# Seven products instead of eight for six of the eight output tiles in each layer's last feed-forward block

## The chip, the core and the metric

The kernel runs on one core of one Trainium2 chip. The metric is the device time of one execution in microseconds (us), lower is better. The engines named below are PE (TensorE, matrix products), DVE (VectorE), ACT (ScalarE), POOL (GpSimd, nearly unused here) and SP (SyncE, which issues the loads).

## The reference

A two-layer encoder trunk over 528 positions (16 meta tokens and 512 frames) of width 1024, all in fp32. Layer 0 mixes by a causal convolution and pooling, layer 1 by gated linear attention. What the change touches is the feed-forward block at the end of each layer and what follows it:

```python
def squared_relu_mlp(u, w1, w2):
    a = jax.nn.relu(u @ w1)
    return (a * a) @ w2
...
        u = rms_norm(h, ffn_norm_g[i])
        h = h + squared_relu_mlp(u, ffn_w1[i], ffn_w2[i])
    return rms_norm(h[:, N_META:], final_norm_g)
```

`ffn_w1` is 1024 x 4096 and `ffn_w2` is 4096 x 1024 in each layer.

## The kernel before

**Products.** Activations lie with channels on the 128 partitions and tokens along the free axis. Each fp32 product is made of three: both operands are split into a high part (rounded to fp32r by ACT) and the rest (a subtraction on DVE), and PE adds hi x lo, hi x hi and lo x hi. One output tile (128 channels) over 1024 input channels is 8 x 3 products. In layer 0 it covers 528 tokens as two matmuls of 264 columns each (48 matmuls); in layer 1 it covers the 512 frames in one matmul (24 matmuls of 512 columns).

**Feed-forward.** The 4096 inner channels are worked in four blocks (`fb` 0 to 3). The first half of a block makes eight tiles of `relu(u @ w1)` (slots `("ffn", layer, fb, 0..7)`), the second half multiplies their squares by the block's part of `w2` and adds the eight result tiles (`8..15`) to `h`. PE writes into four slots of PSUM, `NS = 4`, each of two banks, in the order that `plan_slots` writes out by hand; `start_slot(n)` waits until slot n-4 has been read out.

**Blocks 0 to 2** (`paired_ffn`) take the second half in four pairs of output tiles. A pair is a 2 x 2 block product (two halves of the input channels and tiles by two halves of the tokens) made by seven products instead of eight, Strassen-Winograd. It needs sums of the weights (`pair_sums`, four DVE subtractions or additions into `s_sum`), sums of the squares (`T1` to `T4` beside the four squares `E1, O1, O2, E2`, in `parts8`, split into `c_hi`, `c_lo`), and between the products three copies and a seed on ACT (`seed`, the two `kept` copies, `low`) and three additions into `h` on DVE (`late`, `add_pair` twice). A pair takes 7 x 4 x 3 = 84 matmuls of 264 (layer 0) or 256 columns (layer 1). While PE works on pair p, ACT and DVE split the weights of pair p+1 (`pair_hi`, `pair_lo`, groups 0 to 3); a group's units may be overwritten once PE has done the product that reads them. `parts8` has two buffers, for one pair of first-half tiles each, and ACT's first square of a pair waits for the rests of the pair two before.

**Block 3** (`ffn`) makes all eight result tiles whole, from `a_hi` and `a_lo` (squares, split). After each result tile of layer 0 comes `prep(2, k)`: ACT writes `u_hi` and the squares `h_sq` of the next norm, DVE the rest `u_lo` and the running sum `sq_sum`. In layer 1 ACT's `result` writes `h_sq` and `h` times the final gain into `relu`, PE transposes that tile by four 128 x 128 transposes (`flip_y`), and DVE copies them to `y_tok` (`copy_y`). The last two tiles of layer 1 are made in two halves of 256 tokens each (`end`), followed by the last norm and the output. After layer 0 PE goes on with `project_r` and the first `v` tile, whose weights (`B_V`) are split at the end of block 3.

Every engine runs its instructions in the order in which they are written.

Of the kernel before, what the change touches and what calls it, by code (L numbers as in the profile page):

```python
# [80 lines left out]
PAIRED = FBLK - 1  # L81
# [6 lines left out]
def pair_block(b):  # L88

    first = B_F1 if b >= B_F1 else B_F0  # L90
    return 0 <= b - first < 8 * PAIRED and (b - first) % 8 >= 4

# [12 lines left out]
def plan_slots():  # L105
# [16 lines left out]
    def ffn(layer, norm):  # L122
        for fb in range(FBLK):
            for i in range(2 * KD):
                if layer == 1 and fb == FBLK - 1 and i >= 2 * KD - 2:
                    break
                yield ("ffn", layer, fb, i)
                if fb == 0 and i == 0:
                    yield ("stat", norm)
                if layer == 1 and fb == FBLK - 1 and i > KD:  # L130
                    yield ("y", i - KD - 1)
        if layer == 1:

            yield from (("end", 0, KD - 2), ("y", KD - 3), ("end", 0, KD - 1), ("y", KD - 2, 0),
# [52 lines left out]
def half_freed(n):  # L187


    changed = n // 2 in (B_OUTP, B_OUTP + 1, B_F0, B_F0 + 1, B_V, B_V + 1)  # L190
    return half_reader(n - 4 + (1 - n % 2 if changed else 0))
# [7 lines left out]
def build_trunk(nc, x, meta_tokens, mix_norm_g, ffn_norm_g, ffn_w1, ffn_w2, cp_w_in, cp_conv_w,  # L199
                cp_conv_b, cp_ln_g, cp_ln_b, cp_pool_w, cp_pool_scale, cp_w_out, gla_w_in,  # L200
                gla_gate_w2, gla_gate_b, gla_head_g, gla_w_out, final_norm_g, out):
    with ExitStack() as ctx:
# [9 lines left out]
        h = sb("h", [P, KD, TOK])  # L212
        u_hi = sb("u_hi", [P, KD, TOK], F32R)
# [34 lines left out]
        with ExitStack() as part:  # L248
# [30 lines left out]
            with ExitStack() as last:  # L279
                y_tok = sb("y_tok", [P, TT, D], F32, last)  # L280
# [21 lines left out]
        with ExitStack() as paired:  # L302

            c_hi = sb("c_hi", [P, 7, KD // 2, HALF], F32R, paired)
            c_lo = sb("c_lo", [P, 7, KD // 2, HALF], F32R, paired)
            s_sum = sb("s_sum", [P, 4, KD // 2, P], F32, paired)
            parts8 = sb("parts8", [P, 2, 8, HALF], F32, paired)
# [78 lines left out]
        a_hi_ready = sem("a_hi_ready")  # L386
        a_lo_ready = sem("a_lo_ready")
# [23 lines left out]

        def units(layer, fb):

            return 2 * KD - (2 if layer == 1 and fb == FBLK - 1 else 0)
# [44 lines left out]
        def w_view(t, n):  # L459

            b, j = divmod(n, 2)
            if B_OUTP <= b < B_F0 or B_V <= b < B_K:
                return half_view(t, n)
            return t[:, b % 2, KD * P * j:KD * P * (j + 1)].rearrange("p (k n) -> p k n", k=KD)

        def pair_number(layer, fb, p):
            return 4 * (PAIRED * layer + fb) + p
# [16 lines left out]
        def half_free(eng, n):  # L484

            b = n // 2
            first = B_F1 if b >= B_F1 else B_F0
            fb, i = divmod(n - 2 * first, 16)
            if first <= b < first + 8 * FBLK and fb >= 1 and i < 4:
                pair_group_freed(eng, int(first == B_F1), fb - 1, 3, i)  # L490
# [193 lines left out]
        def _(act):  # L684
# [186 lines left out]
            def paired_ffn(layer, fb, tokens):  # L871
# [3 lines left out]
                block = 2 * (B_F1 if layer else B_F0) + 16 * fb  # L875

# [6 lines left out]
                for i in range(KD):  # L883
# [4 lines left out]
                    count = 4 * (PAIRED * layer + fb) + j  # L888
                    now = parts8[:, j % 2, :, 0:w]
# [5 lines left out]
                    src = relu[:, i % 2, a:b].rearrange("p (t n) -> p t n", t=2)  # L895
                    def part_hi(first, last, t):
# [5 lines left out]
                    if i % 2 == 0:  # L902
                        if count >= 2:
                            act.wait_ge(part_lo_ready, 4 * (count - 1))
                        act.activation(now[:, E1::E2 - E1, :], src, ACT.Square).then_inc(sq_ready, 1)
                        part_hi(E1, T1, 1)
                    else:
# [8 lines left out]
                for p in range(KD // 2):  # L916
# [4 lines left out]
                    def next_hi(g):  # L921
                        if p < KD // 2 - 1:
                            pair_hi(layer, fb, p + 1, g)
                        else:
                            split_hi(block + 16 + g)

                    if p:
# [11 lines left out]

            def ffn(layer, fb, tokens):  # L940
                a, b = tokens
                for i in range(units(layer, fb)):
                    n = SLOT["ffn", layer, fb, i]
                    w = 2 * (B_F1 if layer else B_F0) + 16 * fb + i + 4
                    if i < KD:

                        t = KD * FBLK * layer + KD * fb + i
                        own = KD * layer + i
                        evacuated(act, n)
                        if own >= 2:  # L950

                            act.wait_ge(a_lo_ready, own - 1)
                        act.activation(act2[:, i % 2, a:b], relu[:, i % 2, a:b], ACT.Square)\
                           .then_inc(sq_ready, 1)
                        act.wait_ge(sq_ready, t + 1)
                        act.activation(a_hi[:, i, a:b], act2[:, i % 2, a:b], ACT.Copy)\
                           .then_inc(a_hi_ready, 1)
                    if w < 2 * NB and not (layer == 0 and i == 2 * KD - 1):
                        split_hi(w)
                    if i >= KD and fb == FBLK - 1:  # L960
                        k = i - KD
                        if layer == 0:
                            prep(2, k, n, FULL)
                            if k == KD - 1:
                                split_hi(w)
                            continue
# [1269 lines left out]
```

## Time and profile before

| | |
|---|---|
| median of 3 runs | 1131.76 us (1131.66 to 1132.69) |
| the profiled execution, its own time | 1132.42 us |
| its span, first to last instruction | 1130.6 us (18593 instructions) |
| PE busy | 1112.6 us (98%) |
| DVE busy | 759.5 us (67%) |
| ACT busy | 528.0 us (47%) |
| DMA | 100.39 MB, 89 GB/s mean |

The span leaves 1132.42 - 1130.6 = 1.82 us of the execution's time outside it. PE's matmuls overlap, so the time that a stage costs is read from the starts of its matmuls (the chain of waits merges them), and not from the length of one. A DVE or ACT instruction's listed length also overlaps the next one's start a little: two DVE operations of 528 elements in a row start 0.62 us apart though each is listed with 0.70.

### The profile page before, as it was taken

What the parts mean: (1) busy time and instruction counts of PE and PEld (TensorE: products, weight loads), DVE (VectorE), ACT (ScalarE), POOL (GpSimd) and SP (SyncE); (2) the same over time, 40 slices, a digit from 0 to 9 for tenths busy, and PEclk for the clock granted to TensorE, in tenths of its full rate; (3) what the DMA queues carried; (4) which work ended last, traced back from release to release, by engine and by line L of the source; (5) the groups of instructions that cost most, each with busy time, mean ns of one, the idle gap of its engine ahead of it and who ended that gap; (6) DMA issues with size and microseconds to landing.
All of it is one profiled execution on the core that took longest, in us unless ns stands there. A gap on an engine that the chain in (4) does not pass through costs nothing.

```text
span 1130.6 us, 18593 instructions
## 1 busy us (share of the span) xinstructions
PE 1112.6 (98%) x7759; PEld 1037.0 (92%) x7759; DVE 759.5 (67%) x1072; ACT 528.0 (47%) x830; POOL 2.9 (0%) x30
## 2 busy tenths in 40 slices
PE   7999999999999999999999999999999999999997
PEld 6999999999999999999999788787898898898886
DVE  5898888786786786444663345656786786785443
ACT  7435555454454454332652234534454454454333
POOL 1000000000000000000000000000000000000000
PEclk9999999999999999999999999999999999999999
DMA  7322022133224224232222221132234134133311
GB/s 208 113 75 75 1 76 85 65 107 118 75 78 147 75 75 150 75 113 75 68 83 75 75 76 37 39 112 75 74 113 131 56 113 131 56 113 114 110 38 76
DMA packets 98928, 100.39 MB, mean 89 GB/s; under 512 B 2834, under 2 KB 95692, under 8 KB 98844
## 3 DMA queue, kind: packets, MB, share of 16 engines
q1 hardware_dynamic: 98780, 99.12, 27.8%
q8 instruction: 62, 1.02, 0.4%
q14 instruction: 22, 0.18, 0.0%
q10 hardware_dynamic: 64, 0.07, 0.0%
HBM read 97.09 MB, written 2.10 MB: 88 GB/s over the span
## 4 chain that ended last, share of the span: by engine, by line
PE 97%; DVE 1%; ACT 1%; DMA 0%; issue 0%; ACTq 0%; DVEq 0%
PE ps L1769 62%; PE ps L1955 21%; PE ps L2022 4%; PE ps L1884 3%; PE ps L2103 2%; PE ps L1816 2%; PE ps L2118 1%; PE ps L2052 1%; PE ps L1777 1%; DVE conv L1292 0%; PE ps L2138 0%; DMA xmeta<-in_meta_tokens_dram 0%; PE ps L2129 0%; DVE w_lo L509 0%; ACT w_hi L502 0%
## 5 line engine op out<-in xcount | busy, mean ns | idle before, releaser
L1769 PE MATMUL ps<-u_lo,w_hi 128*128 128x264 f32 (+1 forms) x1120 | 299.8, 323 | 1.7 <-DVE u_lo L1245 1.7
L1769 PE MATMUL ps<-u_hi,w_hi 128*128 128x264 f32 (+1 forms) x1120 | 295.3, 320 | 0.0
L1769 PE MATMUL ps<-u_hi,w_lo 128*128 128x264 f32 (+1 forms) x1120 | 294.8, 319 | 0.0
L502 ACT ACTIVATE w_hi<-raw 128x1024 fp32r<-128x1024 f32 x132 | 138.8, 1055 | 190.4 <-PE ps L1769 180.1
L509 DVE TENSOR_TENSOR w_lo<-raw,w_hi 128x1024 fp32r<-128x1024 f32 x132 | 161.1, 1224 | 97.5 <-ACT w_hi L502 97.3
L1769 PEld LDWEIGHTS ps<-u_lo,w_hi 128*128 128x128 f32 x1120 | 184.9, 189 | 19.8 <-issue 4.7
L1769 PEld LDWEIGHTS ps<-u_hi,w_hi 128*128 128x128 f32 x1120 | 186.1, 188 | 16.3 <-issue 1.2
L1769 PEld LDWEIGHTS ps<-u_hi,w_lo 128*128 128x128 f32 x1120 | 185.7, 189 | 15.4
L1955 PE MATMUL ps<-c_lo,w_hi 128*128 128x264 f32 (+1 forms) x672 | 190.2, 283 | 0.0
L1955 PE MATMUL ps<-c_hi,w_hi 128*128 128x264 f32 (+1 forms) x672 | 190.0, 283 | 0.0
L1955 PE MATMUL ps<-c_hi,w_lo 128*128 128x264 f32 (+1 forms) x672 | 189.9, 283 | 0.0
L1955 PEld LDWEIGHTS ps<-c_hi,w_hi 128*128 128x128 f32 x672 | 126.7, 188 | 0.1
L1955 PEld LDWEIGHTS ps<-c_hi,w_lo 128*128 128x128 f32 x672 | 126.6, 188 | 0.0
L1955 PEld LDWEIGHTS ps<-c_lo,w_hi 128*128 128x128 f32 x672 | 126.5, 188 | 0.1
L1411 DVE SCALAR_TENSOR_TENSOR relu<-ps,rstd 128x528 f32<-128x528 f32 (+1 forms) x64 | 44.7, 699 | 62.3 <-PE ps L1769 62.2
L899 ACT ACTIVATE c_hi<-parts 128x528 fp32r<-128x528 f32 (+1 forms) x96 | 54.1, 581 | 66.9 <-DVE parts L1443 38.3
L1769 PE MATMUL ps<-a_lo,w_hi 128*128 128x264 f32 (+2 forms) x336 | 81.4, 304 | 0.0
L1769 PE MATMUL ps<-a_hi,w_hi 128*128 128x264 f32 (+2 forms) x336 | 80.1, 301 | 0.0
L1769 PE MATMUL ps<-a_hi,w_lo 128*128 128x264 f32 (+2 forms) x336 | 79.8, 299 | 0.0
L1430 DVE TENSOR_TENSOR c_lo<-parts,c_hi 128x528 fp32r<-128x528 f32 (+1 forms) x96 | 60.3, 632 | 22.6 <-ACT c_hi L899 17.7
L548 DVE TENSOR_TENSOR w_lo<-s_sum,w_hi 128x1024 fp32r<-128x1024 f32 x48 | 58.7, 1222 | 9.9 <-ACT w_hi L540 9.5
L1292 DVE SCALAR_TENSOR_TENSOR conv<-conv_in,cw,conv 128x528 f32<-128x528 f32 x79 | 57.5, 766 | 1.1
(251 smaller groups left out, 1518.2 us busy)
## 6 DMA issues: line engine op xcount, KB each, us to landing
raw<-in_ffn_w_dram SPq DMA_DIRECT2D x64, 1024.0 KB, 5.4
raw<-in_gla_w_in_dram SPq DMA_DIRECT2D x12, 1024.0 KB, 5.3
raw<-in_cp_w_in_dram SPq DMA_DIRECT2D x8, 512.0 KB, 5.2
raw<-in_cp_w_out_dram SPq DMA_DIRECT2D x4, 1024.0 KB, 5.1
raw<-in_gla_w_out_dram SPq DMA_DIRECT2D x4, 1024.0 KB, 5.1
xin<-in_x_dram SPq DMA_DIRECT2D x4, 512.0 KB, 5.6
raw<-in_cp_w_in_dram SPq DMA_DIRECT2D x2, 1024.0 KB, 4.9
out_dram<-y_tok SPq DMA_DIRECT2D x4, 512.0 KB, 3.1
```

The costliest lines, as they stand in the source:

```text
L502: act.activation(w_view(w_hi, n), half_view(raw, n), ACT.Copy).then_inc(w_hi_ready, 1)
L509: dve.tensor_tensor(w_view(w_lo, n), half_view(raw, n), w_view(w_hi, n).bitcast(F32), ALU.subtract).then_inc(w_lo_ready, 1)
L548: dve.tensor_tensor(lo, src, hi.bitcast(F32), ALU.subtract).then_inc(w_lo_ready, 1)
L899: act.activation(c_hi[:, first:last + 1, j, 0:w], now[:, first:last + 1, :], ACT.Copy)\
L1292: V.scalar_tensor_tensor(out=conv[:, c, :], in0=src, scalar=wt, in1=conv[:, c, :], op0=ALU.mult, op1=ALU.add).then_inc(tap_done[c], 1)
L1411: V.scalar_tensor_tensor(out=relu[:, i % 2, a:b], in0=slot_ap(n, tokens), scalar=0.0, in1=rstd[:, a:b], op0=ALU.max, op1=ALU.mult)\
L1430: V.tensor_tensor(c_lo[:, first:last + 1, j, 0:w], now[:, first:last + 1, :], c_hi[:, first:last + 1, j, 0:w].bitcast(F32), ALU.subtract)\
L1769: last = mm(ps[:, n % NS, c:c + b - a], l, r[:, a - origin:b - origin], start=(k == 0 and i == 0), stop=(k == count - 1 and i == 2))
L1816: return nc.tensor.transpose(dst, src, ident[0:rows, 0:rows])
L1884: last = mm(ps[:, n % NS, col:col + b - a], l, r[:, a:b], start=(i == mine[0] and m == 0), stop=(i == mine[-1] and m == 2))
L1955: last = mm(bank, l[:, 0, j, :], r, start=(fresh and j == 0 and m == 0), stop=(j == KD // 2 - 1 and m == 2), skip_group_check=not fresh)
L2022: last = mm(ps[:, n % NS, 0:256], l, r, start=(k == 0 and i == 0), stop=(k == KD - 1 and i == 2))
```

## The change

- `PAIRS = [4, 4, 4, 3]`: the last block of each layer now also goes through `paired_ffn`, with three pairs (result tiles 0 to 5). `ffn` is gone.
- Its result tiles 6 and 7 stay whole, but read the squares out of `c_hi`, `c_lo`: `whole_tile` in layer 0, and through `end` in layer 1. For that the last block keeps an eighth part, `E2`, in `c_hi`, `c_lo` (`PARTS = [4, 4, 4, 5]`: one more split on ACT and on DVE for each pair of first-half tiles).
- `prep` (layer 0) and `result` (layer 1) of tiles 2p-2 and 2p-1 are placed inside pair p, by `tile_done`. `flip_y` and `copy_y` take two tiles at a time: `flip_y(0)` on PE after pair 1, `flip_y(1)` after pair 2, `flip_y(2)` after the first `end`; `copy_y(0)` on DVE in pair 2.
- `parts8` has one buffer for all: ACT's first square of a pair of tiles waits for the rests of the pair before.
- The weights of tiles 6 and 7 go where pair 2's units lie and wait for them (`half_free`); the first two `B_V` blocks wait for tile 6 and for tile 7.
- `y_tok` lies elsewhere in SBUF (over `u_hi`).

```diff
-PAIRED = FBLK - 1
+PAIRS = [KD // 2] * (FBLK - 1) + [KD // 2 - 1]
+PARTS = [4] * (FBLK - 1) + [5]
...
-            for i in range(2 * KD):
-                if layer == 1 and fb == FBLK - 1 and i >= 2 * KD - 2:
-                    break
+            last = layer == 1 and fb == FBLK - 1
+            for i in range(2 * KD - (2 if last else 0)):
                 yield ("ffn", layer, fb, i)
...
-                if layer == 1 and fb == FBLK - 1 and i > KD:
-                    yield ("y", i - KD - 1)
+                if last and i == KD + 3:
+                    yield ("y", 0)
...
-            yield from (("end", 0, KD - 2), ("y", KD - 3), ("end", 0, KD - 1), ("y", KD - 2, 0),
+            yield from (("y", 1), ("end", 0, KD - 2), ("y", 2), ("end", 0, KD - 1), ("y", KD - 2, 0),
...
-            parts8 = sb("parts8", [P, 2, 8, HALF], F32, paired)
+            parts8 = sb("parts8", [P, 8, HALF], F32, paired)
...
-            if first <= b < first + 8 * FBLK and fb >= 1 and i < 4:
-                pair_group_freed(eng, int(first == B_F1), fb - 1, 3, i)
+            ffn = first <= b < first + 8 * FBLK
+            if ffn and fb >= 1 and i < 4:
+                pair_group_freed(eng, layer, fb - 1, PAIRS[fb - 1] - 1, i)
+            elif ffn and i >= 8:
+                pair_group_freed(eng, layer, fb, PAIRS[fb] - 1, (0, 3)[i - 14])
+            elif b in (B_V, B_V + 1):
+                filled(eng, SLOT["ffn", 0, FBLK - 1, 14 + b - B_V])
...
                     if i % 2 == 0:
-                        if count >= 2:
-                            act.wait_ge(part_lo_ready, 4 * (count - 1))
+                        act.wait_ge(part_lo_ready, part_count(layer, fb, j))
                         act.activation(now[:, E1::E2 - E1, :], src, ACT.Square).then_inc(sq_ready, 1)
                         part_hi(E1, T1, 1)
+                        if PARTS[fb] == 5:
+                            part_hi(E2, E2, 1)
...
+                def tile_done(k):
+
+                    if fb == FBLK - 1 and k >= 0:
+                        n = SLOT["ffn", layer, fb, KD + k]
+                        if layer == 0:
+                            prep(2, k, n, FULL)
+                        else:
+                            result(k, n, FRAMES, 3 * KD + k)
+
+                for p in range(PAIRS[fb]):
...
                     if p:
                         seed(p)
+                    tile_done(2 * p - 2)
                     act.wait_ge(product_done, 5 * q + 2)
...
+                    tile_done(2 * p - 1)
                     next_hi(0)
...
+                if fb == FBLK - 1:
+                    tile_done(KD - 4)
+                    tile_done(KD - 3)
+                    if layer == 0:
+                        split_hi(2 * B_V)
+                        split_hi(2 * B_V + 1)
+                        tile_done(KD - 2)
+                        tile_done(KD - 1)
+                        split_hi(2 * B_V + 2)
+                        split_hi(2 * B_V + 3)
...
+                def tile_done(k):
+                    if fb == FBLK - 1 and k >= 0:
+                        prep(2 if layer == 0 else 4, k, tokens)
...
-                    if p < KD // 2 - 1:
+                    if p < PAIRS[fb] - 1:
                         pair_sums(layer, fb, p + 1)
+                    tile_done(2 * p - 2)
                     dve.wait_ge(copied, 2 * q + 2)
                     V.tensor_tensor(late, late, kept, ALU.add).then_inc(late_added, 1)
+                    tile_done(2 * p - 1)
+                    if layer == 1 and fb == FBLK - 1 and p == PAIRS[fb] - 1:
+                        copy_y(0)
                     next_lo(0)
...
+                    if layer == 1 and fb == FBLK - 1 and p == 1:
+                        flip_y(0)
+                if fb == FBLK - 1 and layer == 0:
+                    for i in (2 * KD - 2, 2 * KD - 1):
+                        whole_tile(SLOT["ffn", 0, fb, i], 2 * B_F0 + 16 * fb + i,
+                                   ((BANK - w, (E1, O1)), (BANK, (E2, O2))), w)
+
+            def whole_tile(n, half, halves, w):
+
+                start_slot(n)
+                pe.wait_ge(w_lo_ready, group(half) + 1)
+                weights = whalf(half)
+                for k in range(KD):
+                    l_hi, l_lo = weights(k)
+                    for i, (l, c) in enumerate(((l_hi, c_lo), (l_hi, c_hi), (l_lo, c_hi))):
+                        for at, parts in halves:
+                            last = mm(ps[:, n % NS, at:at + w], l, c[:, parts[k % 2], k // 2, 0:w],
+                                      start=(k == 0 and i == 0), stop=(k == KD - 1 and i == 2))
+                last.then_inc(filled_n, 1)
...
+            flip_y(1)
             end(0, KD - 2)
-            flip_y(KD - 3)
+            flip_y(2)
             end(0, KD - 1)
```

## Rows read from the trace of the kernel before

**Rows 1.** The page, busy shares of the engines and granted clock in 40 slices.

```profile
PE 1112.6 (98%) x7759; PEld 1037.0 (92%) x7759; DVE 759.5 (67%) x1072; ACT 528.0 (47%) x830; POOL 2.9 (0%) x30
...
PEclk9999999999999999999999999999999999999999
```

**Rows 2.** Who PE waited for: total us, times, longest; the first and last of eight.

```profile
PE ps L1816 <- DMA gain_rows<-in_mix_norm_g_dram: 5.7, 1, 5.7
...
PE ps L2010 <- DVE u_lo L1176: 0.3, 1, 0.3
```

**Rows 3.** The chain of waits in order: start, length, engine, line, count (us).

```profile
402.13 40.90 PE ps L1955 x336
443.03 93.45 PE ps L1769 x768
...
989.03 39.80 PE ps L1955 x336
1028.84 56.00 PE ps L1769 x240
1084.83 0.44 PE ps L1816 x4
```

**Rows 4.** Timeline of DVE, the seven-product pairs of layer 0's third block.

```profile
415.62 0.69 DVE L562 TENSOR_TENSOR s_sum<-raw 128x512 f32<-128x512 f32 x1
...
418.16 0.70 DVE L1481 TENSOR_TENSOR h<-h,act 128x528 f32<-128x528 f32 x1
419.48 1.23 DVE L548 TENSOR_TENSOR w_lo<-raw,w_hi 128x1024 fp32r<-128x1024 f32 x1 [0.62 <-ACT w_hi L540]
...
422.28 0.70 DVE L1474 TENSOR_TENSOR h<-h,ps 128x528 f32<-128x528 f32 x1
```

**Rows 5.** Timeline of ACT over the same pairs.

```profile
415.33 0.39 ACT L930 ACTIVATE act<-ps 128x264 f32<-128x264 f32 x1 [1.08 <-PE ps L1955]
...
418.31 1.06 ACT L540 ACTIVATE w_hi<-raw 128x1024 fp32r<-128x1024 f32 x1 [1.12 <-PE ps L1955]
```

**Rows 6.** Timeline of DVE, layer 0's last block: one result tile's preparation.

```profile
503.84 0.76 DVE L1176 SCALAR_TENSOR_TENSOR u_lo<-h,vec,u_hi 128x528 fp32r<-128x528 f32 x1
504.52 0.70 DVE L1189 TENSOR_TENSOR sq_sum<-sq_sum,h_sq 128x528 f32<-128x528 f32 x1
```

**Rows 7.** Timeline of PE at the handover to layer 1.

```profile
538.97 0.41 PE L2010 MATMUL ps<-u_hi,rw_both 128*64 128x264 f32 x2
539.69 0.46 PE L2010 MATMUL ps<-u_lo,rw_both 128*64 128x264 f32 x2 [0.32 <-DVE u_lo L1176]
```

**Rows 8.** Timeline of DVE and then ACT, first half of layer 0's third block.

```profile
393.77 0.43 DVE L1430 TENSOR_TENSOR c_lo<-parts,c_hi 128x264 fp32r<-128x264 f32 x1
...
394.47 1.51 DVE L1430 TENSOR_TENSOR c_lo<-parts,c_hi 128x528 fp32r<-128x528 f32 x2
396.33 0.71 DVE L1411 SCALAR_TENSOR_TENSOR relu<-ps,rstd 128x528 f32<-128x528 f32 x1 [0.35 <-PE ps L1769]
...
397.36 0.62 ACT L905 ACTIVATE parts<-relu 128x528 f32<-128x528 f32 x1
```

**Rows 9.** Timeline of DVE, layer 1's third block.

```profile
1004.92 0.69 DVE L1481 TENSOR_TENSOR h<-h,act 128x512 f32<-128x512 f32 x1
1005.95 1.23 DVE L548 TENSOR_TENSOR w_lo<-raw,w_hi 128x1024 fp32r<-128x1024 f32 x1 [0.35 <-ACT w_hi L540]
1007.58 1.23 DVE L548 TENSOR_TENSOR w_lo<-s_sum,w_hi 128x1024 fp32r<-128x1024 f32 x1 [0.40 <-ACT w_hi L540]
1008.72 0.68 DVE L1474 TENSOR_TENSOR h<-h,ps 128x512 f32<-128x512 f32 x1
```

**Rows 10.** Timeline of DVE and then ACT, layer 1's last block.

```profile
1104.99 0.68 DVE L1522 COPY y_tok<-ps 128x512 f32<-128x512 f32 x1
...
1098.27 0.62 ACT L975 ACTIVATE h_sq<-h 128x512 f32<-128x512 f32 x1
1098.79 0.71 ACT L978 ACTIVATE relu<-h,vec 128x512 f32<-128x512 f32 x1
```

More of the change, by code:

```diff
@@ L90, in pair_block @@
     first = B_F1 if b >= B_F1 else B_F0
-    return 0 <= b - first < 8 * PAIRED and (b - first) % 8 >= 4
+    fb, r = divmod(b - first, 8)
+    return 0 <= fb < FBLK and 4 <= r < 4 + PAIRS[fb]
 GROUPS = [0]
@@ L212, in build_trunk @@
         h = sb("h", [P, KD, TOK])
+        with ExitStack() as last:
+            y_tok = sb("y_tok", [P, TT, D], F32, last)
         u_hi = sb("u_hi", [P, KD, TOK], F32R)
@@ L463, in w_view, with part_count, part_order @@
                 return half_view(t, n)
+            if b in (B_F0 + 8 * FBLK - 1, B_F1 + 8 * FBLK - 1) and j == 0:
+                return t[:, 0, 0:KD * P].rearrange("p (k n) -> p k n", k=KD)
             return t[:, b % 2, KD * P * j:KD * P * (j + 1)].rearrange("p (k n) -> p k n", k=KD)
         def pair_number(layer, fb, p):
-            return 4 * (PAIRED * layer + fb) + p
+            return sum(PAIRS) * layer + sum(PAIRS[:fb]) + p
+        def part_count(layer, fb, j):
+            return (sum(PARTS) * layer + sum(PARTS[:fb])) * (KD // 2) + PARTS[fb] * j
+        def part_order(fb, part):
+            order = [(E1, T1), (T2,), (O1, O2), (T3, T4)]
+            if PARTS[fb] == 5:
+                order.insert(1, (E2,))
+            return 1 + [part in names for names in order].index(True)
         def pair_slot(layer, fb, p):
@@ L887, in paired_ffn @@
                     j = i // 2
-                    count = 4 * (PAIRED * layer + fb) + j
-                    now = parts8[:, j % 2, :, 0:w]
+                    count = KD // 2 * (FBLK * layer + fb) + j
                     if i < KD // 2:
@@ L938, in paired_ffn @@
                     next_hi(3)
[L940 to L966, printed above, removed]
-                        result(k, n, FRAMES, 4 * KD - KD + k)
+                if fb == FBLK - 1:
[8 more added lines that the diff above has]
+                        split_hi(2 * B_V + 3)
             def result(k, n, tokens, t):
@@ L981, in ffn_all @@
             def ffn_all(layer, tokens):
-                for fb in range(PAIRED):
+                for fb in range(FBLK):
                     paired_ffn(layer, fb, tokens)
-                ffn(layer, FBLK - 1, tokens)
             ffn_all(0, FULL)
@@ L1727, in _ @@
             end(0, KD - 2)
-            copy_y(KD - 3)
+            copy_y(2)
             end(0, KD - 1)
@@ L1989, in ffn_all, with flip_y @@
             def ffn_all(layer, tokens):
-                for fb in range(PAIRED):
+                for fb in range(FBLK):
                     paired_ffn(layer, fb, tokens)
-                ffn(layer, FBLK - 1, tokens)
-            def flip_y(k):
-                n = SLOT["y", k]
+            def flip_y(i):
+                n = SLOT["y", i]
                 start_slot(n)
-                pe.wait_ge(hg_ready, k + 1)
-                for j in range(TT):
-                    last = flip(ps[:, n % NS, P * j:P * (j + 1)], relu[:, k % 2, META + P * j:META + P * (j + 1)])
+                for k in (2 * i, 2 * i + 1):
+                    pe.wait_ge(hg_ready, k + 1)
+                    for j in range(TT):
+                        c = BANK * (k % 2) + P * j
+                        last = flip(ps[:, n % NS, c:c + P], relu[:, k % 2, META + P * j:META + P * (j + 1)])
```

123 lines of the change are left out of this document (52 added, 71 removed).

## Prediction

> **What bounds the kernel now.** I read the page first, for the engine that is never free: PE is busy for 98% of the span at a granted clock that stays at its full 2.4 GHz, DVE for 67%, ACT less [rows 1]. Busy matmuls overlap, so that alone doesn't say that PE waits for nothing. The list of PE's waits does: eight waits in the whole span, the longest at the start (5.7 us for a load), and the one at the end of layer 0 is 0.3 us [rows 2]. Then the chain of waits in order, where the reader is to see long unbroken pieces of PE through the feed-forward blocks, and only there [rows 3]. So in these stages a matmul removed is time removed, one for one, as long as DVE and ACT keep delivering what PE asks for. The rest of the work is to find where they might not, and for that I laid the new order of instructions over the timelines of a block that already runs in pairs [rows 4, 5, 9].
>
> **Fewer matmul columns: the main term.** In layer 0 a pair takes 40.90 / 4 = 10.23 us and a whole tile 93.45 / 16 = 5.84 us, so two tiles 11.68 us [rows 3]. Three pairs save 3 x 1.46 = 4.37 us. In layer 1 a pair takes 39.80 / 4 = 9.95 us and a whole tile 56.00 / 10 = 5.60 us, so two tiles 11.20 us [rows 3]. Three pairs save 3 x 1.25 = 3.75 us. The last two tiles take the same matmuls as before (48 a tile in layer 0, four `end` pieces of 24 in layer 1), only with their squares out of other tiles: nothing. Sum 8.12 us, all on the path. The count of matmuls goes up, not down: each pair of layer 0 has 84 for 96, each of layer 1 has 84 of 256 columns for 48 of 512, which is -36 + 108 = +72.
>
> The Trainium skill ("TensorE: Matmul & The Clock Gate", Back-to-back issue gap) gives the spacing of warm matmuls as the columns by 2.4 GHz plus 2.5 ns. That would be an estimate of 109 ns for 256 columns, 112.5 for 264 and 216 for 512; the rows here show 118, 122 and 233 ns. By the page's figures the same counts would save 3 x 1.35 + 3 x 1.19 = 7.6 us instead of 8.1. The rows are of this very stage, so I keep them.
>
> **First half of the last block.** It takes over what blocks 0 to 2 do there, and a fifth part for each pair of tiles. There PE doesn't wait in any of the six blocks [rows 2]. The fifth part is one more copy on ACT and one more subtraction of 264 columns on DVE, 0.43 us at most [rows 8], four times a layer. DVE waits 0.35 us for PE at each such point [rows 8], and after a tile PE has three more slots of 5.84 us before it wants this one back. Taken at nothing; without that cover it would be 8 x 0.43 = 3.4 us.
>
> **One buffer for the parts.** ACT's first square of a pair of tiles now waits for the last rests of the pair before. That square already waits for DVE's `relu`, and on DVE the rests stand ahead of the `relu`. In the rows the last two rests end at 395.98, the `relu` begins at 396.33, the square at 397.36 [rows 8]. So the new wait is over 1.4 us before the old one ends. Nothing queues behind it that doesn't queue already. Nothing.
>
> **Layer 0, preparations inside the pairs.** This is the tight place. DVE has, between its first sum for the next pair (415.62) and the end of that pair's work, hardly a gap: the largest shown is 0.62 us before the first weight split [rows 4]. To this come for the two tiles of the pair before 2 x 0.68 us for `u_lo` (503.84 to 504.52), 0.62 for a sum of squares (0.70 listed) and about 0.35 for the first one, which is a copy [rows 6]. Laid over pair 1: the sums end at 418.16; u_lo 0.68 and copy 0.35, the late addition 0.62, u_lo 0.68 and sum 0.62 end at 421.11; the first split of pair 2's weights, 1.23 long, ends at 422.34 where before it ended at 420.71 [rows 4]. PE wants it when it begins pair 2, at 402.13 + 2 x 10.23 = 422.58 [rows 3]. It is 0.2 us in time. The second split ends near 423.5 and is wanted one product (1.46 us) after the start, at 424.0. In pair 2 DVE has no sums to make (2.54 us less) and catches up. ACT has the room: after the seed it idles 1.08 us up to the first `kept` copy at 415.33, and again 1.12 us before the first weight copy at 418.31 [rows 5]; into each gap go two operations, some 1.2 us with their overlap, which push what follows by about 0.1 us. Of the moved steps none issues a load, and POOL has no part. SP's loads wait for the splits: the block with tiles 6 and 7 is released once pair 1's weights are split, just ahead of the sums at 415.62, and wanted after pair 2's fourth product, at 428.4. Taken at nothing, with 0.4 us as the next value if the estimate of one DVE operation is off by as much.
>
> **The weights of tile 6** wait for pair 2's fourth product, three products (4.4 us) before the end of the pair, and a copy and a split take 1.06 + 1.23 us [rows 4, 5]. Those of tile 7 wait for the end of pair 2 and have a tile (5.84 us). Nothing.
>
> **The handover to layer 1.** Before, PE lost time here: two steps of `project_r` lie 0.72 us apart and not 0.24, for the `u_lo` of tile 6 [rows 7], because ACT split weights for `v` first. After, tiles 0 to 5 are prepared before tile 7 begins, and tile 6 while PE makes tile 7. I take the whole 0.48 us as a gain. The first `v` weights wait for tile 6 instead of an earlier tile; both halves are split about 5.4 us after tile 6's end, and PE, after tile 7 and seven steps of `project_r` (3.4 us), asks for them at 9.3 us.
>
> **Layer 1, the slots.** `flip_y(0)` stands between pair 1 and pair 2, with eight transposes for 0.88 us (0.44 for four [rows 3]); six tiles' transposes are the same in number, so this costs nothing by itself. But its slot shifts the order by one: pair 2's second slot is now the one that pair 1's first result is added from. Laid over block 2, pair 1 ends at 989.03 + 2 x 9.95 = 1008.93 and the transposes at 1009.81. The addition begins at 1008.72 [rows 9]. DVE's added copy and sum, 0.35 + 0.60 us, come before the first split: 1004.92 + 0.35 + 2 x 0.60 = 1006.47 instead of 1005.95. The second split then begins at 1007.60 instead of 1007.58, since DVE had waited before both [rows 9]. The addition, 0.68 long, ends at 1009.4, in time by 0.4 us.
>
> **Layer 1, the tail.** `flip_y(2)` wants `h` times gain of tiles 4 and 5. After pair 2's end ACT splits tile 7's weights (1.06) and does two rounds of 0.53 + 0.60 us (0.62 and 0.71 listed [rows 10]), ready at 3.4 us; PE comes there after 0.88 + 2.84 = 3.72 us (24 matmuls of 256 at 0.1185 [rows 3]). `copy_y(1)`, 2 x 0.60 us on DVE [rows 10], ends before its slot is wanted. From the second `end` on all is as before.
>
> **Sum.** 8.12 + 0.48 = 8.60 us. The profiled execution took 1132.42 us (span 1130.6 and 1.82 around it), so its counterpart would take 1123.8 us with a span of 1122.0. It lies 0.66 us above the median of 1131.76 us; the median becomes 1123.2 us.
>
> **The rivals.** (1) DVE comes late. For it speaks that three of the margins above are 0.2 to 0.4 us. If the added operations take their listed lengths (2 x 0.76 + 2 x 0.70) and the 0.62 us idle stays, the split of layer 0 ends at 418.16 + 0.70 + 2.92 + 0.62 + 1.23 = 423.6, 1.1 us late; the same in layer 1, and 0.4 us at each of the two transposes, gives 3.0 us. So 0.4 to 3.0 us are given back: 1123.6 to 1126.2, middle 1124.9 us. Against it: pair 2 has no sums, so it can't add up from pair to pair. (2) A load comes late: the last block's loads wait for splits that move later, and one that lands after its use stops ACT, then PE. Against it are 7 us and more of margin at each. One miss would cost some 2 to 5 us, 1125 to 1128 us. (3) Slower: the single buffer makes ACT's squares wait in all 32 pairs of tiles. It decides at 10.9 / 32 = 0.34 us of PE's time each; at the length of one square, 0.62 us [rows 8], it would be 19.8 us, 1143 us. Against it is the order on DVE above, and three free slots. (4) The change doesn't do what it says, if the last block's pairs weren't 1.25 to 1.46 us shorter than two tiles. The rows of the pairs are of the same code with the same shapes, so there is nothing for it: under 1 in 100.
>
> **Chances.** Forecast 0.79 (1122.6 to 1123.8), late DVE 0.15, late load 0.03, slower 0.02, the rest 0.01. A difference under 0.2%, 2.3 us, can't be told from none in this kernel: faster 0.96, same 0.01, slower 0.03. The range takes the forecast, with the spread of the runs below it, and most of the late DVE: 1122.5 to 1125.8 us.
>
> **What would show it.** In the profile after: some 7831 matmuls on PE for 7759; three pairs of 10.2 us in place of six tiles of 5.84 at the end of layer 0, three of 9.95 in layer 1; no wait of PE before `project_r`. Rival 1 would be a PE wait for `w_lo` (L548) or for `h` (`add_pair`) at the start of the last block's pair 2, or before the third transposes. Rival 3 would be ACT idle before its even squares with DVE's `c_lo` as releaser, in all blocks. The forecast is wrong if PE waits more than 0.7 us in sum in the two last blocks.

## The result, and the profile after

The changed kernel takes 1122.97 us (median of 6 runs, 1122.74 to 1123.48) where the kernel before takes 1132.11 us beside it (6 runs, 1131.66 to 1132.69): 0.992 of it, 95% interval 0.9908 to 0.9932, some 9.1 us less. Its profiled execution took 1123.48 us, 8.94 less than that of before.

The page of the changed kernel, head and busy times; it stands against [rows 1].

```profile
span 1121.7 us, 18932 instructions
...
PE 1103.9 (98%) x7831; PEld 1035.2 (92%) x7831; DVE 809.2 (72%) x1170; ACT 555.7 (50%) x890; POOL 2.9 (0%) x30
...
PEclk9999999999999999999999999999999999999998
```

The 72 matmuls that were counted are there. PE's share stays 98%: its work and the span shrink together. DVE has 50 us more.

The chain of waits of the changed kernel in order (start, length, engine, line, count); it stands against [rows 3].

```profile
226.85 40.74 PE ps L1969 x336
...
401.79 40.74 PE ps L1969 x336
442.53 46.72 PE ps L1784 x384
489.25 30.74 PE ps L1969 x252
519.99 11.71 PE ps L2005 x96
531.69 3.40 PE ps L2032 x28
535.09 2.48 PE ps L2044 x21
...
540.19 8.57 PE ps L2044 x72
...
1068.40 19.93 PE ps L1969 x168
1088.33 0.87 PE ps L1831 x8
1089.20 9.93 PE ps L1969 x84
```

L1784 is the first half of a block, L1969 the pairs, L2005 `whole_tile` and `end`, L2032 `project_r`, L2044 the `v` tiles, L1831 the transposes. The table sets the stages against each other; a stage is the distance between two starts of the chain.

| stage | before | after | difference |
|---|---|---|---|
| layer 0, second half of the last block | 46.73 | 30.74 + 11.71 = 42.45 | -4.28 |
| layer 0, end of tile 7 to the long `v` piece | 9.04 | 540.19 - 531.69 = 8.50 | -0.54 |
| layer 1, end of the last first half to the third of the four `end` pieces | 42.16 | 38.43 | -3.73 |
| layer 0, the pairs of blocks 0 to 2, which the change doesn't reorder | 3 x 40.90 | 3 x 40.74 | -0.48 |
| all else | | | +0.06 |

The sum is -8.97 us, and the chain's last piece starts 8.97 us earlier too (1116.15 for 1125.12). The rest of +0.06 is mostly the long `v` piece, 8.57 us for 8.49. The two pieces of the chain of before that the table uses and [rows 3] lacks, and behind them the second one's counterpart after:

```profile
545.52 8.49 PE ps L2022 x72
...
1115.80 2.84 PE ps L1769 x24
...
1106.83 2.84 PE ps L2005 x24
```

PE's list of waits (total us, times, longest), against [rows 2], has seven entries for eight. The one before `project_r` is gone, and none is for the pairs or for `whole_tile`; the first and the last of the changed kernel:

```profile
PE ps L1831 <- DMA gain_rows<-in_mix_norm_g_dram: 5.8, 1, 5.8
...
PE ps L1831 <- DVE h L1238: 0.4, 1, 0.4
```

That list leaves out small losses: a matmul is listed with 0.28 us and more while the next starts 0.12 us after it, so its modelled end lies beyond the next one's start. A start 0.2 us late, in the run e11 below, isn't listed either. So I also read the starts. Timeline of DVE and then of PE in the changed kernel, at the start of layer 0's pair 2, the place that the prediction called tight; the DVE rows stand against [rows 4].

```profile
504.67 0.69 DVE L580 TENSOR_TENSOR s_sum<-raw,s_sum 128x512 f32<-128x512 f32 x1
505.28 0.76 DVE L1185 SCALAR_TENSOR_TENSOR u_lo<-h,vec,u_hi 128x528 fp32r<-128x528 f32 x1
505.96 0.43 DVE L1195 COPY sq_sum<-h_sq 128x528 f32<-128x528 f32 x1
506.30 0.70 DVE L1500 TENSOR_TENSOR h<-h,act 128x528 f32<-128x528 f32 x1
506.92 0.77 DVE L1185 SCALAR_TENSOR_TENSOR u_lo<-h,vec,u_hi 128x528 fp32r<-128x528 f32 x1
507.60 0.70 DVE L1198 TENSOR_TENSOR sq_sum<-sq_sum,h_sq 128x528 f32<-128x528 f32 x1
508.21 1.22 DVE L561 TENSOR_TENSOR w_lo<-raw,w_hi 128x1024 fp32r<-128x1024 f32 x1
...
509.37 0.28 PE L1969 MATMUL ps<-c_hi,w_lo 128*128 128x264 f32 x1
509.58 0.36 PE L1969 MATMUL ps<-c_lo,w_hi 128*128 128x264 f32 x1
509.78 0.28 PE L1969 MATMUL ps<-c_hi,w_hi 128*128 128x264 f32 x1
```

DVE has no gap from its sums to the split, which ends at 509.43. PE's starts are 0.12 us apart until 509.37, then 0.21 and 0.20: the pair begins 0.09 us late and its second matmul takes 0.08 more. That is the 0.17 or 0.18 us by which the three pairs (30.74) are over 3/4 of an earlier block of the same kernel (3/4 of 40.74 is 30.56).

### The profile page after: what moved, and what is told of

Same layout as the page of the kernel before. It is cut to its first block, busy times and chain, and to the rows that moved or that the text cites. A ratio compares the mean times of both kernels' runs of the same rounds, so it can differ in the third digit from the quotient of the medians.

```text
span 1121.7 us, 18932 instructions
## 1 busy us (share of the span) xinstructions
PE 1103.9 (98%) x7831; PEld 1035.2 (92%) x7831; DVE 809.2 (72%) x1170; ACT 555.7 (50%) x890; POOL 2.9 (0%) x30
## 4 chain that ended last, share of the span: by engine, by line
PE 97%; DVE 1%; ACT 1%; DMA 0%; issue 0%; ACTq 0%; DVEq 0%
PE ps L1784 54%; PE ps L1969 27%; PE ps L2044 4%; PE ps L1899 3%; PE ps L2005 2%; PE ps L2125 2%; PE ps L1831 2%; PE ps L2140 1%; PE ps L2074 1%; PE ps L1792 1%; DVE conv L1301 0%; PE ps L2160 0%; PE ps L2032 0%; DMA xmeta<-in_meta_tokens_dram 0%; PE ps L2151 0%; DVE w_lo L522 0%
## 5 line engine op out<-in xcount | busy, mean ns | idle before, releaser
L1784 PE MATMUL ps<-u_lo,w_hi 128*128 128x264 f32 (+1 forms) x1120 | 299.9, 323 | 1.7 <-DVE u_lo L1254 1.7
L1784 PE MATMUL ps<-u_hi,w_hi 128*128 128x264 f32 (+1 forms) x1120 | 295.5, 320 | 0.0
L1784 PE MATMUL ps<-u_hi,w_lo 128*128 128x264 f32 (+1 forms) x1120 | 295.0, 319 | 0.0
L1969 PE MATMUL ps<-c_lo,w_hi 128*128 128x264 f32 (+1 forms) x840 | 238.2, 284 | 0.0
L1969 PE MATMUL ps<-c_hi,w_hi 128*128 128x264 f32 (+1 forms) x840 | 237.3, 282 | 0.0
L1969 PE MATMUL ps<-c_hi,w_lo 128*128 128x264 f32 (+1 forms) x840 | 237.1, 282 | 0.0
L1784 PEld LDWEIGHTS ps<-u_lo,w_hi 128*128 128x128 f32 x1120 | 185.0, 189 | 19.7 <-issue 4.7
L1784 PEld LDWEIGHTS ps<-u_hi,w_hi 128*128 128x128 f32 x1120 | 186.1, 188 | 16.3 <-issue 1.2
L1784 PEld LDWEIGHTS ps<-u_hi,w_lo 128*128 128x128 f32 x1120 | 185.6, 189 | 15.3
L1969 PEld LDWEIGHTS ps<-c_lo,w_hi 128*128 128x128 f32 x840 | 158.3, 188 | 0.3
L1969 PEld LDWEIGHTS ps<-c_hi,w_hi 128*128 128x128 f32 x840 | 158.4, 189 | 0.2
L1969 PEld LDWEIGHTS ps<-c_hi,w_lo 128*128 128x128 f32 x840 | 158.2, 188 | 0.0
L913 ACT ACTIVATE c_hi<-parts 128x528 fp32r<-128x528 f32 (+3 forms) x136 | 74.6, 571 | 89.4 <-DVE parts L1452 51.6
L1439 DVE TENSOR_TENSOR c_lo<-parts,c_hi 128x528 fp32r<-128x528 f32 (+3 forms) x136 | 83.2, 620 | 30.1 <-ACT c_hi L913 23.8
L553 ACT ACTIVATE w_hi<-s_sum 128x1024 fp32r<-128x1024 f32 x60 | 63.6, 1059 | 14.4 <-PE ps L1784 10.9
L553 ACT ACTIVATE w_hi<-raw 128x1024 fp32r<-128x1024 f32 (+1 forms) x60 | 50.7, 845 | 38.3 <-PE ps L1969 29.8
L561 DVE TENSOR_TENSOR w_lo<-raw,w_hi 128x1024 fp32r<-128x1024 f32 (+1 forms) x60 | 57.3, 954 | 9.3 <-ACT w_hi L553 9.3
```

The source lines that it names most:

```text
L553: act.activation(hi, src, ACT.Copy).then_inc(w_hi_ready, 1)
L561: dve.tensor_tensor(lo, src, hi.bitcast(F32), ALU.subtract).then_inc(w_lo_ready, 1)
L913: act.activation(c_hi[:, first:last + 1, j, 0:w], now[:, first:last + 1, :], ACT.Copy)\
L1439: V.tensor_tensor(c_lo[:, first:last + 1, j, 0:w], now[:, first:last + 1, :], c_hi[:, first:last + 1, j, 0:w].bitcast(F32), ALU.subtract)\
L1784: last = mm(ps[:, n % NS, c:c + b - a], l, r[:, a - origin:b - origin], start=(k == 0 and i == 0), stop=(k == count - 1 and i == 2))
L1969: last = mm(bank, l[:, 0, j, :], r, start=(fresh and j == 0 and m == 0), stop=(j == KD // 2 - 1 and m == 2), skip_group_check=not fresh)
```

## The experiments

All are timed against the kernel before, on the same chip; differences of a few tenths are read in the traces, where a stretch of pairs repeats to about 0.02 us and the handover to 0.05. The start of the first long stretch of products differs by up to 1.1 us between the profiled executions (15.15 to 16.24), so whole times carry that too. Where a time is set against the changed kernel's 1122.97 us, the two were not taken side by side, and the stages decide.

### Does the single buffer cost anything, and does it do anything to blocks 0 to 2?

Theory: it costs nothing. Rival 3: up to 0.34 us and more for each of 32 pairs. Beside that, the 0.16 us a block that nobody had asked for is to be placed.

`e1_one_buffer`, the kernel before with the single buffer alone:

```diff
-            parts8 = sb("parts8", [P, 2, 8, HALF], F32, paired)
+            parts8 = sb("parts8", [P, 8, HALF], F32, paired)
...
-                        if count >= 2:
-                            act.wait_ge(part_lo_ready, 4 * (count - 1))
+                        act.wait_ge(part_lo_ready, 4 * count)
```

> The kernel before with one buffer for the squares' parts, nothing else. By my theory the new wait of ACT's square ends 1.4 us before the wait that it has anyway: the time of before within 0.1 us, no new PE wait, ACT's squares where they were. Rival (single buffer costs PE): 0.34 us or more for each of the 24 pairs of tiles here, 8 us slower. If the 0.16 us by which each paired block of layer 0 got shorter in the changed kernel comes from the buffer, this kernel is 0.48 us faster.

Measured: 1132.5 us for 1132.16, ratio 1.0002 (0.9993 to 1.0011). The buffer costs nothing, rival 3 falls. The chain shows layer 0's pairs as before, so the buffer isn't what shortened them:

```profile
226.65 40.91 PE ps L1954 x336
```

`e2_eight_parts_lie` is e1 with the changed kernel's layout and no other instruction:

```diff
-            c_hi = sb("c_hi", [P, 7, KD // 2, HALF], F32R, paired)
-            c_lo = sb("c_lo", [P, 7, KD // 2, HALF], F32R, paired)
+            c_hi = sb("c_hi", [P, 8, KD // 2, HALF], F32R, paired)
+            c_lo = sb("c_lo", [P, 8, KD // 2, HALF], F32R, paired)
```

> As e1, and c_hi and c_lo are allocated with eight parts though only seven are used: no instruction changes, only where c_lo and what lies behind it lie. If the unforeseen 0.16 us in each paired block of layer 0 (40.74 us for 40.90) comes from the place of c_lo, this kernel has 40.74 us there and is 0.5 us faster than e1. If it comes from anything else of the change, it equals e1.

Measured: 1131.92 us for 1132.16, ratio 0.9998 (0.9989 to 1.0006), which alone decides nothing. The chain does:

```profile
226.10 40.74 PE ps L1954 x336
```

So does that of the two other blocks. The same 336 matmuls take 0.16 us less because their operands lie elsewhere in SBUF. Two more kernels ask which array it is. `e8_c_lo_moved` gives only `c_hi` the eighth part, which moves `c_lo` and all behind it up by 4224 bytes a partition; `e9_behind_moved` gives it only to `c_lo`, which leaves `c_hi` and `c_lo` and moves what is behind.

```diff
-            c_hi = sb("c_hi", [P, 7, KD // 2, HALF], F32R, paired)
+            c_hi = sb("c_hi", [P, 8, KD // 2, HALF], F32R, paired)
             c_lo = sb("c_lo", [P, 7, KD // 2, HALF], F32R, paired)
```

> The kernel before with one parts buffer, and c_hi alone allocated with eight parts: c_lo and all behind it move up by 4224 bytes a partition. If the place of c_lo makes layer 0's paired blocks 40.74 us for 40.91, they are 40.74 here; if it is the size or the place of what lies behind c_lo, they are 40.91 here or in between.

```diff
             c_hi = sb("c_hi", [P, 7, KD // 2, HALF], F32R, paired)
-            c_lo = sb("c_lo", [P, 7, KD // 2, HALF], F32R, paired)
+            c_lo = sb("c_lo", [P, 8, KD // 2, HALF], F32R, paired)
```

> The kernel before with one parts buffer, and c_lo alone allocated with eight parts: c_lo stays, s_sum and parts8 move up by 4224 bytes. If the place of c_lo is the cause, layer 0's paired blocks stay at 40.91 us; if the place of s_sum or parts8 is, they are 40.74.

Measured: e8 1131.68 us (0.9994, 0.9984 to 1.0004), e9 1133.02 us (1.0002, 0.9992 to 1.0011), both beside 1132.63. One row of the chain of e8, then of e9:

```profile
226.31 40.74 PE ps L1954 x336
...
226.45 40.91 PE ps L1954 x336
```

The place of `c_lo` decides; that of `s_sum` and `parts8` doesn't. Why a moving operand at one place goes faster than at another no run here shows, nor whether it is the place itself that counts or the distance from `c_hi`, which changes with it.

### Is the handover what I took it for?

Theory: before, `u_lo` of tile 6 stood behind a `v` split on ACT and DVE, and the order alone is worth the 0.5 us. Rival: the gain comes from somewhere else in the new last block.

`e3_handover_order`, the kernel before with the preparation of tile 6 ahead of that split:

```diff
-                    if w < 2 * NB and not (layer == 0 and i == 2 * KD - 1):
+                    swap = layer == 0 and fb == FBLK - 1 and i == 2 * KD - 2
+                    if w < 2 * NB and not (layer == 0 and i == 2 * KD - 1) and not swap:
                         split_hi(w)
...
-                            if k == KD - 1:
+                            if k >= KD - 2:
                                 split_hi(w)
```

> The kernel before, with the preparation of layer 0's tile 6 placed ahead of the split of the v weights that waits for tile 7. By my theory PE's 0.3 us wait in project_r goes, and 0.5 us of the span with it. Rival (the preparation was late for its own length): the wait stays or moves to tile 7's u_lo, no gain.

Measured: 1132.03 us for 1132.16, ratio 0.9999 (0.999 to 1.0008). The time alone can't resolve half a microsecond here. The chain can:

```profile
535.75 3.39 PE ps L2012 x28
...
544.24 8.56 PE ps L2024 x72
```

544.24 - 535.75 = 8.49 us where before it was 9.04, and the wait for `u_lo` is gone from PE's list. So all of the changed kernel's 0.54 us comes with this order alone, and it needs no pair. The long `v` piece behind it takes 8.56 us here for 8.49; up to its end 0.47 us are gained (17.06 for 17.53), and 0.46 in the changed kernel.

### How tight is DVE in the last blocks?

Theory: at the start of pair 2 DVE is at PE's pace in layer 0 and has about 0.4 us in layer 1; any more work there is paid in full. Rival: the 0.17 us has another cause (a load, ACT, the new slot), and DVE has room.

`e4_dve_dose`, the changed kernel with two needless subtractions of 528 or 512 columns on DVE in pair 1 of each last block:

```diff
                     tile_done(2 * p - 1)
+                    if fb == FBLK - 1 and p == 1:
+                        for at in range(2):
+                            V.tensor_tensor(now[:, 2 * at:2 * at + 2, :], now[:, 4:6, :], now[:, 6:8, :], ALU.subtract)
```

> The changed kernel with two more DVE subtractions of 528 (layer 0) or 512 elements (layer 1) in the last block's pair 1, between the preparations and the first weight split of pair 2; their results are read by nobody. That is 1.24 and 1.20 us. Theory (DVE now reaches the start of pair 2 together with PE): layer 0 takes nearly all of it, 1.2 us, layer 1 what is over its slack of some 0.3 us, 0.9 us: 2.1 us slower than the changed kernel. Rival (PE alone bounds the last block, DVE has room to spare as its 72% busy share suggests): no change.

Measured: 1125.25 us, 0.9936 (0.9924 to 0.9949), 2.28 us more than the changed kernel. Timeline of DVE and of PE in layer 0, then of DVE and of PE in layer 1:

```profile
507.45 1.32 DVE L1504 TENSOR_TENSOR parts<-parts 128x528 f32<-128x528 f32 x2
508.69 1.22 DVE L561 TENSOR_TENSOR w_lo<-raw,w_hi 128x1024 fp32r<-128x1024 f32 x1
...
508.61 0.28 PE L1972 MATMUL ps<-c_hi,w_lo 128*128 128x264 f32 x1
510.05 0.36 PE L1972 MATMUL ps<-c_lo,w_hi 128*128 128x264 f32 x1 [1.17 <-DVE w_lo L561]
...
1086.24 1.28 DVE L1504 TENSOR_TENSOR parts<-parts 128x512 f32<-128x512 f32 x2
1087.44 1.22 DVE L561 TENSOR_TENSOR w_lo<-raw,w_hi 128x1024 fp32r<-128x1024 f32 x1
...
1089.71 0.68 DVE L1492 TENSOR_TENSOR h<-h,ps 128x512 f32<-128x512 f32 x1
...
1088.60 1.03 PE L1834 MATMUL ps<-ident,relu 128*128 128x128 f32 x8
1090.49 0.36 PE L1972 MATMUL ps<-c_lo,w_hi 128*128 128x256 f32 x1 [0.85 <-issue]
```

In layer 0 the dose holds DVE for 508.69 - 507.45 = 1.24 us, and PE's gap grows from 0.21 (509.37 to 509.58 in the changed kernel) to 1.44: by 1.23, all of it. In layer 1 the dose is 1.20 us, and from the transposes' start to the pair's it is 1.89 us for 0.79 (1088.17 to 1088.96 in the changed kernel, below): 1.10 are paid. It is the slot that is late there: the addition that frees it ends at 1090.39, 0.10 us ahead of the pair's first matmul, while the first weight split had ended at 1088.66. The room was 0.1 us there and not the 0.3 and 0.4 of the expectation and the prediction, and the expected 0.9 for layer 1 was low by 0.2. Both layers together pay 2.33 us in the trace.

`e5_dve_prepares_later`, the changed kernel with DVE's preparations of tiles 0 and 1 at the end of pair 1, behind all that pair 2 waits for:

```diff
-                    tile_done(2 * p - 2)
+                    if p != 1:
+                        tile_done(2 * p - 2)
...
-                    tile_done(2 * p - 1)
+                    if p != 1:
+                        tile_done(2 * p - 1)
...
                     next_lo(3)
+                    if p == 1:
+                        tile_done(0)
+                        tile_done(1)
```

> The changed kernel with DVE's part of the preparations of tiles 0 and 1 moved from the middle of pair 1 to its end, behind the weight splits for pair 2. Theory: the two starts of 0.20 us instead of 0.12 at pair 2 of layer 0 go, 0.17 us less there, and no new wait, since pair 2 has no sums to make. Rival (DVE is short over the whole block, not at one place): the wait comes back at pair 2's end or at tile 6, no gain or a loss of 1 us.

Measured: 1123.07 us, 0.9916 (0.9903 to 0.993). In the chain the three pairs take 0.17 us less than 30.74, and no start at pair 2 is late:

```profile
488.55 30.57 PE ps L1974 x252
```

The loss was DVE's order, and this removes it. The median doesn't show 0.17 us.

`e6_less_pe`, the changed kernel with 6 of 84 matmuls of each pair of the last blocks left out, so that PE asks sooner:

```diff
-                        for j in range(KD // 2):
+                        for j in range(KD // 2 - (2 if fb == FBLK - 1 and part == T3 else 0)):
```

> The changed kernel with half of one of the seven products (S3 times T3, 6 of 84 matmuls) left out of each pair in the two last blocks, so part of the computation is missing. If PE alone bounds those blocks, it gains 3 x 0.73 + 3 x 0.71 = 4.3 us. By my theory DVE runs without a pause from the start of the block's second half to pair 2's weights, whatever PE does: of layer 0 only pair 2's 0.73 us is gained, of layer 1 pair 2's 0.71 and its slack of some 0.3 us, together 1.7 to 1.8 us.

Measured: 1121.88 us, 0.9907 (0.9892 to 0.9923), 1.09 less than the changed kernel's 1122.97. By stages it is 1.54 less: in the trace the three pairs of layer 0 take 518.51 - 488.50 = 30.01 us for 30.74 (-0.73) and layer 1's, with their transposes, 29.92 for 30.73 (-0.81). The matmuls left out are worth 36 x about 0.12 = 4.3 us, so 1.5 of it comes through, what the third pair alone has and layer 1's 0.1 us of room. PE's rows at the start of pair 2:

```profile
507.52 0.28 PE L1970 MATMUL ps<-c_hi,w_lo 128*128 128x264 f32 x1
508.82 0.36 PE L1970 MATMUL ps<-c_lo,w_hi 128*128 128x264 f32 x1 [1.02 <-DVE w_lo L561]
```

Pair 1 of layer 0 starts late as well (0.39 us between two starts for 0.12), and PE's list has both waits for `w_lo`, 1.2 us together. Two pairs of three are now bound by DVE as much as by PE: fewer matmuls there bring next to nothing, though the page gives DVE 72%.

### Is there a fourth pair in it?

Layer 0's tiles 6 and 7 are still whole: 11.71 us for a pair's 10.19. By that, a fourth pair is worth 1.5 us, if DVE can carry its sums and splits. Layer 1 was left as it is, since its last two tiles go through the halves of `end`. Three kernels share this core:

```diff
-PAIRS = [KD // 2] * (FBLK - 1) + [KD // 2 - 1]
+PAIRS = ([KD // 2] * FBLK, [KD // 2] * (FBLK - 1) + [KD // 2 - 1])
...
                         elif fb < FBLK - 1:
                             split_lo(block + 16 + g)
+                        elif layer == 0:
+                            if g < 2:
+                                split_lo(2 * B_V + g)
```

They differ in where DVE prepares the finished tiles. `e10_fourth_pair_plain` leaves them where the changed kernel has them. `e7_fourth_pair` puts tiles 0, 1 and 3 at the end of their pairs:

```diff
-                    tile_done(2 * p - 2)
+                    if p != 1:
+                        tile_done(2 * p - 2)
...
-                    tile_done(2 * p - 1)
+                    at_end = (2 * p - 2,) * (p == 1) + (2 * p - 1,) * (p == 1 or (p == 2 and layer == 0))
+                    if not at_end:
+                        tile_done(2 * p - 1)
...
+                    for k in at_end:
+                        tile_done(k)
```

> The changed kernel with all four pairs of layer 0's last block by seven products (no fifth part there), the v weights split behind pair 3's fourth product and end, and DVE's preparations spread so that none stands ahead of a weight split where it would be late: tiles 0 and 1 at the end of pair 1, tile 3 at the end of pair 2. Theory (PE sets the time as long as DVE's splits are in time): tiles 6 and 7 take 10.19 us for 11.71, 1.5 us less, and 0.17 us less at pair 2's start: 1.7 us faster than the changed kernel, 1121.3 us, no PE wait at the handover (u_lo of tile 6 some 0.5 us in time). Rival (tiles 6 and 7 now end together with the block and their preparation is bare): a PE wait of 1 us or more in project_r, no gain.

> As e7, but with DVE's preparations where the changed kernel has them, ahead of and behind the late addition. Theory: DVE carries its lag from pair 1 into pair 2, where it now has sums to make as well, so pair 3 starts 0.8 us late and pair 2 0.17 us late: some 1.0 us slower than e7. Rival (there is slack again by pair 3): as e7 within 0.2 us.

Measured: e7 1122.37 us (0.991, 0.9895 to 0.9925), e10 1123.03 us (0.9914, 0.9899 to 0.9929). In the trace the second half of layer 0's last block takes 41.64 us in e7 and 41.73 in e10, for 42.45: 0.8 and 0.7 gained, not 1.7. Both expectations missed. The plain order, e10, is late where it was said to be, by 0.10 us at pair 2 and 0.74 at pair 3; what was wrong is that e7 would be in time. In e7 it is the start of the new pair that is late:

```profile
519.02 0.28 PE L1978 MATMUL ps<-c_hi,w_lo 128*128 128x264 f32 x1
519.94 0.36 PE L1978 MATMUL ps<-c_lo,w_hi 128*128 128x264 f32 x1 [0.64 <-DVE w_lo L563]
```

And DVE, a pair earlier, stands idle where the preparations had been:

```profile
504.73 0.70 DVE L1508 TENSOR_TENSOR h<-h,act 128x528 f32<-128x528 f32 x1
506.02 1.23 DVE L563 TENSOR_TENSOR w_lo<-raw,w_hi 128x1024 fp32r<-128x1024 f32 x1 [0.59 <-ACT w_hi L555]
507.70 1.23 DVE L563 TENSOR_TENSOR w_lo<-s_sum,w_hi 128x1024 fp32r<-128x1024 f32 x1 [0.45 <-ACT w_hi L555]
```

DVE waits 1.04 us for ACT's splits there, and the work it put off then falls into pair 2, which with a fourth pair behind it has sums of its own. Work moved away from one deadline had moved onto the next.

`e11_fourth_pair_spread` fills those gaps: from e7, tile 0's preparation back ahead of the late addition, tile 2's behind the first two splits of pair 2.

```diff
-                    if p != 1:
+                    if not (p == 2 and layer == 0):
                         tile_done(2 * p - 2)
...
-                    at_end = (2 * p - 2,) * (p == 1) + (2 * p - 1,) * (p == 1 or (p == 2 and layer == 0))
+                    at_end = (2 * p - 1,) * (p == 1 or (p == 2 and layer == 0))
...
                     next_lo(1)
+                    if p == 2 and layer == 0:
+                        tile_done(2 * p - 2)
```

> As e7, but tile 0's preparation is back ahead of the late addition in pair 1, where DVE in e7 stood waiting for ACT (0.59 and 0.45 us), and tile 2's is moved behind the first two weight splits of pair 2. Theory: DVE's first split for pair 3 then ends before PE wants it (in e7 it was 0.8 us late), layer 0's last four pairs take 40.8 us (41.64 in e7), and with 42.45 us for the same work in the changed kernel this one is 1.6 us faster than the changed kernel. Rival (DVE is over its limit in sum and the wait only moves): the 0.8 us turn up at the v weights or at u_lo.

`e12_changed_again` is the changed kernel unaltered, on the same chip:

> The changed kernel once more, unaltered, beside e11 on the same chip. By the theory 1.6 us slower than e11; with the same 0.17 us late start of layer 0's pair 2. Rival: equal to e11 within 0.3 us.

Measured: e11 1121.8 us (1121.23 to 1122.26; 0.9906, 0.9889 to 0.9923), e12 1123.17 us (1122.74 to 1124.0; 0.9918, 0.9904 to 0.9933). That is 1.37 us less, and the two don't overlap. The chain of e11:

```profile
488.79 40.74 PE ps L1980 x336
529.53 2.90 PE ps L2038 x24
...
538.26 8.49 PE ps L2050 x72
```

Four pairs take 40.74 us, as in an earlier block, for 42.45. The handover takes 538.26 - 529.53 = 8.73 for 8.50, as a `u_lo` comes 0.2 us late, so a small part of the rival came true. Net -1.48 us. By its median this is the fastest of the kernels here that compute the whole result. In e12 the late start stands again, with the same two starts of 0.22 and 0.19 us (508.65, 508.87, 509.06), so it belongs to the kernel and not to one execution.

## Why the prediction was right, and where it wasn't

It gave 1123.2 us and the kernel takes 1122.97; the profiled executions differ by 8.94 us where the sum was 8.60. That the median is met to 0.2 us is in part luck: the sum was taken off a median of 1131.76 us, and beside the changed kernel the kernel before has 1132.11, so that 9.1 us were saved for 8.60. Two errors hide in the sum, one of each sign.

**The main term** was 4.37 and 3.75 us. Measured: 4.28 and 3.73 in their places, the first with the 0.17 us late start in it. The rows of the pairs that already ran were the right prices, since shapes and code are the same.

**The tight place of layer 0** was given as 0.2 us in time and was 0.1 late. The order of DVE's work was right to the operation, and its length too: from the first `u_lo` (505.28) to the end of the split (509.43) it took 4.15 us for the 4.18 laid out. What failed is the clock against which it was held. I took PE's demand from the chain of waits, which starts a piece where the matmul before is taken to end, and DVE's from the timeline. The block of before that I read starts at 402.13 in the chain and at 401.97 in the timeline. The changed kernel's starts at 489.25 in the chain and, in the timeline, at 489.09:

```profile
489.09 0.28 PE L1969 MATMUL ps<-c_lo,w_hi 128*128 128x264 f32 x1
```

The demand came 0.16 us sooner than I read it, and from the end of the split to the matmul another 0.15 us pass (509.43 to 509.58). Of the 0.2 us nothing is left. **The slot in layer 1** went by the same step: 0.4 us foreseen, 0.1 by the dose. DVE and PE at that place in the changed kernel:

```profile
1088.10 0.68 DVE L1492 TENSOR_TENSOR h<-h,ps 128x512 f32<-128x512 f32 x1
...
1088.17 1.03 PE L1831 MATMUL ps<-ident,relu 128*128 128x128 f32 x8
1088.96 0.36 PE L1969 MATMUL ps<-c_lo,w_hi 128*128 128x256 f32 x1
```

The addition ends at 1088.78, 0.42 us ahead of the chain's 1089.20, as foreseen (0.41), but only 0.18 ahead of the matmul's start.

So **rival 1**, late DVE, is the right mechanism at a small size: 0.17 us for the 0.4 to 3.0 given. Its harsher reading, listed lengths and the old idle time added up, is refuted: `u_lo` listed with 0.76 takes 0.68 us to the next start, a sum listed with 0.70 takes 0.61, and the idle time was swallowed.

**The handover** was 0.48 and measured 0.54 up to the long `v` piece, 0.46 with that piece; e3 has 0.55 and 0.47 from the order alone. Shown.

**What was taken at nothing**: the single buffer (e1: nothing, and rival 3 falls), the fifth part in the first half (46.72 us for 384 matmuls against half of 93.45, and no wait), tile 6's weights (its tile starts on the beat), and the loads (rival 2: no wait for one in either last block). The second transposes of layer 1's tail came in time: 2.87 us for the 24 matmuls ahead of them, where the term had 2.84.

**What wasn't in the sum at all** is the 0.48 us in blocks 0 to 2. I priced the change of layout by its waits and gave it nothing. It moves `c_lo`, and with it the spacing of 1008 matmuls. The sum's own terms came to 4.28 + 3.73 + 0.54 = 8.55 us for 8.60, and all else gave back 0.06, mostly in the long `v` piece, which isn't explained: e1, which has none of the new pairs, shows 8.57 us there too. So the forecast was 0.1 us too good on what it had reasoned about and 0.5 us short of what it hadn't seen.

**Left open**: why the place of `c_lo` matters (itself or its distance from `c_hi`), and why it does in layer 0's blocks and hardly in layer 1's, which take 39.80 to 39.82 us before and 39.82 to 39.83 after.

## What to carry to other kernels

Price a change of form by rows of the same form elsewhere in the trace, and then look for the engine that must feed it: here its busy share of 72% said nothing, a gapless run up to one deadline said all, and a dose of needless work measured the room to 0.1 us. Compare demand and supply on one clock, from starts in the timeline, since the chain's pieces began 0.16 to 0.24 us later than their first matmul here. And put moved work into the gaps in which an engine waits, not merely behind a deadline: the fourth pair brought 0.8 us by the one and 1.5 by the other.

## What I hadn't expected of the hardware

The place of a matmul's moving operand in SBUF changes its pace. With `c_lo` 4224 bytes a partition further on, 336 matmuls of 264 columns take 40.74 us for 40.91 (121.3 ns for 121.8 each) in e2, e8 and the changed kernel, and 40.90 to 40.92 in before, e1, e3 and e9; the streams of 256 columns in layer 1 hardly move (39.77 to 39.80 us for 336 in e2 and e8, 39.82 or 39.83 in the changed kernel and e9). The place isn't all: e7 has `c_lo` where the changed kernel has it and shows 40.78 us in each of the three blocks, which is open. And a matmul of a pair that had to wait is followed by the next only 0.20 us later, where the stream has 0.12 (0.20 in e4, e6 and e7 as well): a stop of 0.09 us costs 0.17.
